# Layer 0's down weights in one run of 16 KB for each partition, with every fourth gate and up column loaded to match

## What is computed

```python
def expert_block(args):                       # one block of tokens, one of 32 experts
    xb, e = args
    hmid = jax.nn.silu(xb @ e_gate[e]) * (xb @ e_up[e])      # [tokens, 1024] @ [1024, 512]
    return hmid @ e_down[e]                                  # [tokens, 512] @ [512, 1024]
```

## Time and profile before

| what | us |
|---|---|
| median of 3 runs | 2613.81 |
| the profiled execution | 2615.54 |
| its span | 2614.0 |
| TensorE matmul busy in the span | 2423.8 |
| DMA queue q1 (weights), share of 16 engines over the span | 55.9% |
| expert loop of layer 0, in the span | 948.26 to 1476.10 |
| expert loop of layer 1, in the span | 2101.89 to about 2586 |

### The profile page before, as it was taken

The page is one execution under the profiler, slowest core; times in us unless marked ns, Lnnn a source line. Parts: engine busy times, 40 slices in busy tenths (PEclk is TensorE's granted clock), DMA queues, the critical chain, the costliest instruction groups (busy, mean ns, idle before and its releaser), DMA issues.

```text
span 2614.0 us, 45378 instructions
## 1 busy us (share of the span) xinstructions
PE 2423.8 (93%) x19002; PEld 1433.1 (55%) x19003; DVE 1023.2 (39%) x2380; ACT 502.1 (19%) x999; POOL 231.1 (9%) x392
## 2 busy tenths in 40 slices
PE   6999999999999989999999999999999998888885
PEld 2445545454444467776667455577677454444442
DVE  1226546366574343222222342436557522211122
ACT  2023222222231011111011212223222111111111
POOL 3000001000000011111111100000000011111111
PEclk8999999999999999999999999999999899999997
DMA  9111118243344389999999742133466789999993
GB/s 309 65 65 65 49 62 301 98 139 97 109 120 143 129 317 404 409 401 394 385 381 377 271 145 73 65 113 93 169 190 202 281 351 417 419 424 419 421 399 138
DMA packets 139739, 614.87 MB, mean 235 GB/s; under 512 B 16241, under 2 KB 20881, under 8 KB 118961
## 3 DMA queue, kind: packets, MB, share of 16 engines
q1 hardware_dynamic: 114946, 558.01, 55.9%
q0 software_dynamic: 24688, 55.41, 6.7%
HBM read 596.41 MB, written 42.11 MB: 244 GB/s over the span
## 4 chain that ended last, share of the span: by engine, by line
PE 66%; DMA 23%; DVE 7%; issue 2%; ACT 1%; POOL 0%; SPq 0%; DVEq 0%; POOLq 0%; ACTq 0%
DMA ring<-in_e_down_dram 21%; PE bank L1504 12%; PE bank L1358 11%; PE bank L1348 7%; PE bank L1774 6%; PE bank L1517 5%; PE score_banks L1791 4%; PE score_banks L1811 3%; PE bank L1675 2%; PE score_banks L1553 2%; PE score_banks L1796 2%; PE bank L1766 2%; PE bank L1577 2%; PE turned_banks L1563 2%; PE bank L1682 1%
## 5 line engine op out<-in xcount | busy, mean ns | idle before, releaser
L1504 PE MATMUL bank<-HT,ring 128*128 128x512 f32 (+1 forms) x1024 | 340.9, 488 | 0.9 <-ACT scr L1048 0.4
L1358 PE MATMUL bank<-ring,HT 128*128 128x512 f32 (+1 forms) x800 | 295.4, 526 | 0.0
L1774 PE MATMUL bank<-scr,ring 128*64 128x80 f32 x7936 | 282.6, 233 | 5.2 <-issue 4.0
L1774 PEld LDWEIGHTS bank<-scr,ring 128*64 128x64 f32 x7936 | 276.8, 137 | 18.9 <-issue 18.9
L1766 PE MATMUL bank<-ring,scr 128*64 128x256 f32 x1984 | 242.5, 396 | 39.0 <-DMA ring<-in_e_gate_dram 25.8
L1504 PEld LDWEIGHTS bank<-HT,ring 128*128 128x128 f32 x1024 | 191.3, 191 | 123.6 <-issue 111.6
L1358 PEld LDWEIGHTS bank<-ring,HT 128*128 128x128 f32 x800 | 149.8, 191 | 132.0 <-issue 126.1
L1766 PEld LDWEIGHTS bank<-ring,scr 128*64 128x64 f32 x1984 | 139.1, 137 | 142.6 <-DMA ring<-in_e_gate_dram 44.0
L1348 PE MATMUL bank<-HT,ring 128*128 128x512 f32 (+1 forms) x512 | 197.6, 546 | 1.9 <-ACT HT L1048 1.9
L1811 PE MATMUL score_banks<-ring,scr 128*64 128x512 f32 x512 | 125.4, 635 | 26.1 <-DMA ring<-in_e_down_dram 24.6
L1348 PEld LDWEIGHTS bank<-HT,ring 128*128 128x128 f32 x512 | 98.3, 194 | 92.1 <-issue 88.2
(11 more groups left out here) (292 smaller groups left out, 2688.0 us busy)
## 6 DMA issues: line engine op xcount, KB each, us to landing
ring<-in_e_down_dram SPq DMA_DIRECT2D x64, 2048.0 KB, 26.9
ring<-in_e_up_dram SPq DMA_DIRECT2D x62, 2048.0 KB, 27.4
ring<-in_e_gate_dram SPq DMA_DIRECT2D x62, 2048.0 KB, 27.0
ring<-in_w_in_dram SPq DMA_DIRECT2D x34, 2048.0 KB, 7.9
ring<-in_w_mod_dram SPq DMA_DIRECT2D x32, 1024.0 KB, 5.2
ring<-in_w_mod_dram SPq DMA_DIRECT2D x8, 2048.0 KB, 16.0
ys<-consts POOLq DMA_DIRECT2D x1, 10240.0 KB, 36.4
ring<-in_w_branch_dram SPq DMA_DIRECT2D x4, 2048.0 KB, 7.7
```

Of the source, the lines that this page charges most:

```text
L1358: m = pe.matmul(bank[:, 0:width], HT[:, k, t * P:t * P + P], w[:, k, 0:width], start=k == 0, stop=k == KT_D - 1)
L1504: m = pe.matmul(bank[:, 0:NQ], w[:, k, (ft % 4) * P:(ft % 4) * P + P], HT[:, k, 0:NQ], start=k == 0, stop=k == KT_D - 1)
L1774: m = pe.matmul(ps[bank][rows_, f * cap:f * cap + cap], w[:, k, f * P + hf * HALF:f * P + hf * HALF + HALF], XTv[:, k, :], start=k == 0, s ...
```

## The change

Layer 0 reads its down weights by the same view as layer 1, in the loop's loads and in the overflow loop's. Partition p then holds the rows 4p to 4p + 3, so the hidden feature on partition p in group f must be 4p + f. `hidden` therefore takes every fourth column of gate and up: for the half hf the 64 columns hf * 256 + f, hf * 256 + f + 4, and so on.

```diff
-                    src = src.rearrange("a (p k) n -> p (a k) n" if c < 2 or TILED[l] else "a (k p) n -> p (a k) n", p=P)
+                    src = src.rearrange("a (p k) n -> p (a k) n", p=P)
                     sp.dma_start(slot_view(3 * par + c, 512 if c < 2 else D), src).then_inc(w_full[3 * par + c], 16)
...
-                                    order = "a (p k) n -> p (a k) n" if c < 2 or TILED[l] else "a (k p) n -> p (a k) n"
-                                    src = ins[w][l, bass.ds(e, 1)].rearrange(order, p=P)
+                                    src = ins[w][l, bass.ds(e, 1)].rearrange("a (p k) n -> p (a k) n", p=P)
                                     pool.dma_start(dst, src).then_inc(ov_w[c], 16)
...
                                 m = pe.matmul(ps[bank][rows_, f * cap:f * cap + cap],
-                                              w[:, k, f * P + hf * HALF:f * P + hf * HALF + HALF], XTv[:, k, :],
+                                              w[:, k, hf * 256 + f:hf * 256 + 256:4], XTv[:, k, :],
                                               start=k == 0, stop=k == KT_D - 1)
```

## The result

The changed kernel takes 2792.78 us (median of 4 runs, 2791.41 to 2793.68) against 2614.61 us before (4 runs beside them): a ratio of 1.068, 95% interval 1.067 to 1.069. It is 178 us slower, where the text above forecast 14 us faster. The time lies outside the stated range, and what came is rival (c).

A forecast was written before the change was run, and what follows sets the result against it. The prediction took TensorE, then late down weights in layer 0's expert loop, to bound the kernel. A 13.7 us gain from 16 KB packets and nothing for strided loads gave 2600.1 us from 2613.8, range 2587 to 2613.

The forecast's parts named there:

- rival (c): Gate and up products, L1774: weight loads twice as long, 58 ns, set TensorE's pace; 162 us more, 2776 us; chance 0.16.
- What bounds the kernel: Layer 0's expert loop: TensorE sets the pace at first, then waits for down weights from the 14th expert, 24.2 us.
- the picture of stock and slack: Layer 0's loop: down loads fall behind 1.45 us per expert; TensorE waits once 17.4 us of slack is gone.
- The strided weight loads: Gate and up products, L1774: 60 to 62 ns per load against 70 available, so hidden behind matmuls and costing nothing.
- The rule named beside it: Skill's cacheline note, for L1774's loads: reads within a 16-byte line run at full rate, each new line pays; no size.
- The down load's price: Layer 0's down loads: 4 KB packets cost 0.47 us per expert over 16 KB ones; removing them gains 13.7 us.
- my lower bound at 0.3: Two down and up loads ahead of each loop: 16 KB packets save 0.3 us per expert, a gain of 8.6 us.
- my working gives: Layer 0's loop: lag 0.98 us per expert, slack lasts 17.8 experts, 9.2 wait 1.14 us each, 10.5 us left.
- All waits go: Layer 0's loop: loads run as in layer 1, TensorE sets the pace throughout, 24.2 us gained, 2589.6 us; chance 0.22.
- the packets are not the cause: Layer 0's loop: gathered rows hold the DMA engines at 17.0 us per expert, time stays 2613.8 us; chance 0.12.

The follow-up runs named there:

- runs of the distances and of the transposes: The kernel before, with products in the last four experts changed to other column distances, or to transposes, one-tile and 80-partition products; distance 4 took 61 ns a record.

## Why the prediction was wrong, point by point

**What bounds the kernel** was read right: the runs of 16 KB moved the waits as the picture of stock and slack says. One reading in it was loose: the landings show 17.0 us for an expert in the first window, but there q1 moved an expert's 6.29 MB in 140 x 6.29 / 55.32 = 15.9 us. The landings fell behind faster than the bytes; whether by slower ones among the 16 engines or by loads that share them is not shown.

**The strided weight loads are the step that failed.** "I cost the stride at nothing, hidden behind the matmuls" went by the loads of the token transposes, 60 ns for 64 columns, and by the moving operand of layer 1. The first belong to a kind of load that hardly pays for gaps, as the transposes at distances 4 and 8 show. The second takes two floats of every four, which is two in each 16 bytes, as at the distance of 2 that stayed hidden. Neither row was a product's load that steps into new 16 bytes with each column. Such loads take 121 ns on a tile, against the 60 to 62 of my working and the 70 that the matmuls leave.

**The slower rival (c)** had the place and nearly the price: loads twice as long, 58 ns, an expert of 21.4 us and 162 us in all. Measured are 60.6 ns, 22.00 us and 178 us; it got 16 in 100. Its argument, two tiles that load with gaps at once, was not the reason: one tile alone takes as long, 122 ns. The rule named beside it needs no second tile, and it was right against the row that I set against it.

**The down load's price** had the right sign and twice the size. The same measure taken inside layer 0, with the runs of 16 KB alone, from 1000 to 1140 us, is

```profile
q1 hardware_dynamic: 3823, 55.71, 96.4%
```

0.964 x 140 us for 55.71 MB, 15.24 us for 6.29 MB against 15.47: **0.23 us**, not 0.47. The runs of the distances and of the transposes have the transfers of before there and give 15.54 and 15.46 us, so the difference is larger than the spread between runs. My 15.00 us was layer 1's, which gathers fewer rows, and by one run gathers stretch the loads a little: without them the same measure in layer 0 is 0.987 x 140 us for 56.69 MB, 15.34 us instead of 15.47. The lightly loaded pair, my lower bound at 0.3, was the nearer row. With 0.23 my working gives 17.4 / 1.22 = 14.3 experts of slack and 12.7 that wait 1.38 us, 17.5 us; 24.2 - 17.5 = 6.7 us, and 6.6 were measured.

**All waits go** (rival a) and **the packets are not the cause** (rival b) each hold a part of the truth: packets cost 0.23 us, and without the gathers no wait for a weight is left in layer 0. Rival (b) had put the whole difference down to the rows; the 16 KB runs alone gained 6.6 us.

## What to carry to other kernels

Before a layout is changed for longer DMA runs, ask which operand pays for it: a stationary operand of a float32 product whose columns lay 4, 5 or 8 floats apart loaded at about half its contiguous rate, while 2 apart was free here. So shorten the runs until two columns share 16 bytes: the runs of 8 KB gained 4 to 5 us where those of 16 KB gained 6.6 (the intervals overlap). And price a new access pattern by a row of the same kind of instruction; a transpose is not a product.

## What was not expected

- Transposes load columns with gaps at 116 to 123 ns for 128 columns, products at 232 to 239 ns.
- In the run of distances TensorE's clock fell to its lower level (granted 0.50, 1.2 GHz) some 5 us after it had begun the full-width loads, one every 232 ns. The strided loads did not slow down with it, (8.26 - 0.33) / 34 = 233 ns, and up's contiguous ones behind them, (13.13 - 0.33) / 60 = 213 ns, were only 9% faster. The rows are the timeline of the weight loads from 1471.8 to 1479.8 and from 1480.5 to 1493.2 us, both at 0.50:

```profile
1471.67 8.26 PEld L1774 LDWEIGHTS bank<-scr,ring 128*128 128x128 f32 x35
...
1480.24 13.13 PEld L1774 LDWEIGHTS bank<-scr,ring 128*128 128x128 f32 x61
```

- Gathers of some 32 rows of 4 KB for an expert in layer 0, and 16 in layer 1, cost 47 us in all (one run), though all of queue q0 takes 3.9% to 5.6% of the DMA engines in layer 0 and 2.3% in layer 1.
